# RWKV products stacked in a hybrid encoder layer: b and k in one stationary operand, u and v in one, v centred as it is turned

## The chip, the cores and the metric

The kernel runs on one core of a Trainium2 chip. The metric is the time on the device in microseconds (us) from start to end of one execution of the program; lower is better. The engines are TensorE (PE in the rows, its weight loads PEld), VectorE (DVE), ScalarE (ACT), GpSimd (POOL) and SyncE (SP).

## The reference

One layer of an encoder over 512 tokens of width 2048: a projection feeds three mixers (banded attention, an RWKV-7 time mixing over 16 heads of 64 features, sliding attention with sinks), whose outputs are joined by a projection; then cross attention into 256 tokens and an MLP of width 8192. The change touches the time mixing alone:

```python
def step(state, inp):
    r_t, w_t, k_t, v_t, a_t, b_t = inp
    sa = jnp.einsum('bhij,bhj->bhi', state, a_t)
    state = state * w_t[:, :, None, :] + sa[..., None] * b_t[:, :, None, :] + v_t[..., None] * k_t[:, :, None, :]
    return state, jnp.einsum('bhij,bhj->bhi', state, r_t)
...
y = wkv7_scan(rh, split_heads(decay, B_HEADS), kh, vh, -kk, kk * ah.astype(jnp.float32))
mean = jnp.mean(y, axis=-1, keepdims=True)
var = jnp.mean(jnp.square(y - mean), axis=-1, keepdims=True)
y = ((y - mean) * lax.rsqrt(var + B_GN_EPS)).reshape(b, s, c).astype(pr.dtype) * ln_w + ln_b
bonus = jnp.sum(rh * kh * r_k, axis=-1, keepdims=True) * vh
return (y + bonus.reshape(b, s, c)) * g, v
```

## The kernel before

The large projections are done as three fp32r products (high and low parts) of 128x128 weights with 512 tokens, L1141 to L1143. The input projection runs in 15 groups of 8 units; a unit is 256 rows of the weights. For each unit ScalarE makes the high part (`w_hi`), VectorE the low part (`w_lo`, L713), two units ahead of TensorE. Each group gives three tiles of 128 features in banks 0 to 2 of PSUM. Groups 3 to 10 give r, k and v of a pair of heads (8 pairs, two heads of 64 in the two halves of the partitions).

The RWKV work of the pairs is laid by hand between these products, in the same instruction streams. A unit has three thirds, so a group has 24 positions p. In group g three stages run: `elem` for the pair q = g - 4, `chain` for the pair before it (c), `fin` for the one before that (f). `position(p, g)` issues what belongs to p on each engine, and the engines follow their own streams in order. Ahead of the position's work TensorE issues the chain's step of that third, and behind it six dense matmuls (two tiles, three products each).

`elem` works on chunks of 64 tokens (NC = 8) in fp32. All its small products go through `both` (L1157): the same 64x64 block for the two heads, on the two diagonal quarters of the array; `grams` and `to_tokens` repeat it for 8 chunks. Positions on TensorE: 0 decay and gate projections with 64 rows each (L1189, L1190), 3 turning of v, 8 the bonus sum (L1220), 9 turning of k, 10 gram of k and a, 11 gram of k and r, 12 two grams of a and b, 13 turning of b, 14 gram of b and r and the first product of a blocked inverse, whose levels fill positions 14 to 23 (t, x, xT). VectorE's positions: 6 k decayed (L843) and r decayed, 7 and 8 two reciprocals, `a_dec` (L855), 9 and 10 b (L858, L861), 10 the bonus times v (L866, it frees bank 5 by `bon_ev`), 11 and 12 four masks (L783), 13 start of the inverse, and for `fin` a reciprocal (L887).

`chain` has three steps in a unit: z (L1262, first third, up to two `both`), u (second third, one), then state and y (L1279, last third: two for the new state, then y from u, from v and from the old state). Between them ScalarE copies z and u (L576, L580) and VectorE updates the state (L959, L962). y gathers in bank 7 over the 8 units.

`fin` copies y (L558), takes the mean over a head by a product with a constant (L1194, position 1), subtracts it on VectorE (L819, position 2), squares, takes the variance (L1211) and a gate (L1213, L1214, position 5); GpSimd scales and stores the tile.

After the groups come the attentions, the output projections and the MLP, which the change leaves as they are.

## Time and profile before

| | |
|---|---|
| median of 3 runs | 2764.14 us (2763.07 to 2765.19) |
| profiled execution | 2762.59 us |
| its span, first to last instruction | 2760.9 us |
| mean granted TensorE clock | 0.996 |
| TensorE busy | 2712.9 us, 98% |
| VectorE busy | 1236.4 us, 45% |
| ScalarE busy | 809.3 us, 29% |

The groups with RWKV work take 75.8 us each, from about 143 us to about 820 us. Starts of instructions are in us from the span's start. A matmul's recorded time overlaps with those of its neighbours, so starts are compared. An fp32 matmul shows as two instructions (two passes), each with its own weight load; four small ones in a row ("x4") are the two passes for both heads of one chunk.

### The profile page before, as it was taken

The numbers are of one execution on the slowest core, as the hardware profiler recorded it, in microseconds if no ns is written. First come the engines' busy times: TensorE is split into PE (matmuls) and PEld (weight loads), VectorE is DVE, ScalarE is ACT, GpSimd is POOL, SyncE is SP. The second block draws the span as 40 slices with busy tenths as digits, with TensorE's granted clock in tenths as the row PEclk, the third lists the DMA queues.
The fourth block names the chain that finished last, engine by engine and source line by source line (L and its number), as shares of the span: only waits on it lengthen the run. The fifth ranks groups of instructions, "written<-read, shape, count | busy, mean of one in ns | idle before, by whom it ended". The sixth has DMA issues, their size and how long they took to land.

```text
span 2760.9 us, 44373 instructions
## 1 busy us (share of the span) xinstructions
PE 2712.9 (98%) x18368; PEld 2158.3 (78%) x18368; DVE 1236.4 (45%) x1895; ACT 809.3 (29%) x1333; POOL 132.9 (5%) x237
## 2 busy tenths in 40 slices
PE   9999999999998999998999999999999999999997
PEld 7877777777777766786888888888888888888885
DVE  6266666666435545344433333333333333333333
ACT  5222222222124444243431221312213222122222
POOL 4000111001121100000000000000000000000000
PEclk9999999999999999999999999999999999999998
DMA  4311111111135422221233223322323323323322
GB/s 162 119 60 49 48 48 52 45 50 50 59 108 197 170 79 62 84 88 51 86 98 99 95 97 99 97 93 99 98 92 99 99 92 98 99 92 98 99 94 112
DMA packets 72396, 249.23 MB, mean 90 GB/s; under 512 B 8960, under 2 KB 9088, under 8 KB 71104
## 3 DMA queue, kind: packets, MB, share of 16 engines
q1 hardware_dynamic: 65232, 222.62, 25.3%
q0 software_dynamic: 7024, 24.56, 2.6%
q8 instruction: 109, 1.79, 0.3%
q14 instruction: 31, 0.25, 0.0%
HBM read 236.93 MB, written 10.22 MB: 90 GB/s over the span
## 4 chain that ended last, share of the span: by engine, by line
PE 94%; DVE 3%; issue 1%; DMA 1%; ACT 1%; DVEq 0%; SPq 0%; POOL 0%; ACTq 0%
PE ps L1141 28%; PE ps L1143 26%; PE ps L1142 26%; PE ps L1159 9%; PE ps L1375 1%; PE ps L1354 1%; PE ps L1363 1%; DMA h<-in_mem_turned 1%; PE ps L1153 1%; DVE w_lo L713 0%; PE ps L1214 0%; PE ps L1205 0%; PE ps L1194 0%; PE ps L1211 0%; PE ps L1220 0%
## 5 line engine op out<-in xcount | busy, mean ns | idle before, releaser
L713 DVE TENSOR_TENSOR w_lo<-w_raw,w_hi 128x1024 fp32r<-128x1024 f32 (+2 forms) x440 | 506.0, 1150 | 1143.4 <-ACT w_hi L432 1143.4
L432 ACT ACTIVATE w_hi<-w_raw 128x1024 fp32r<-128x1024 f32 (+2 forms) x440 | 439.0, 998 | 1539.3 <-PE ps L1143 1531.4
L1141 PE MATMUL ps<-act_hi,w_hi 128*128 128x512 f32 x1792 | 730.1, 407 | 1.1 <-DVE w_lo L713 1.1
L1143 PE MATMUL ps<-act_hi,w_lo 128*128 128x512 f32 x1792 | 700.1, 391 | 0.0
L1142 PE MATMUL ps<-act_lo,w_hi 128*128 128x512 f32 x1792 | 699.2, 390 | 0.0
L1141 PE MATMUL ps<-w_hi,mid_hi 128*128 128x512 f32 x1088 | 424.4, 390 | 1.4 <-DVE mid_lo L1087 1.4
L1143 PE MATMUL ps<-w_hi,mid_lo 128*128 128x512 f32 x1088 | 423.3, 389 | 0.0
L1142 PE MATMUL ps<-w_lo,mid_hi 128*128 128x512 f32 x1088 | 423.3, 389 | 0.0
L1141 PEld LDWEIGHTS ps<-act_hi,w_hi 128*128 128x128 f32 x1792 | 336.2, 188 | 93.7 <-issue 12.0
L1143 PEld LDWEIGHTS ps<-act_hi,w_lo 128*128 128x128 f32 x1792 | 336.5, 188 | 72.1
L1142 PEld LDWEIGHTS ps<-act_lo,w_hi 128*128 128x128 f32 x1792 | 336.8, 188 | 68.9 <-issue 6.0
L1141 PEld LDWEIGHTS ps<-w_hi,mid_hi 128*128 128x128 f32 x1088 | 204.3, 188 | 43.5 <-DVE mid_lo L1087 1.6
L1143 PEld LDWEIGHTS ps<-w_hi,mid_lo 128*128 128x128 f32 x1088 | 204.3, 188 | 42.4
L1142 PEld LDWEIGHTS ps<-w_lo,mid_hi 128*128 128x128 f32 x1088 | 204.3, 188 | 41.9
L1020 DVE SCALAR_TENSOR_TENSOR h<-ps,rq,h 128x512 f32<-128x512 f32 x128 | 87.2, 744 | 104.9 <-PE ps L1143 104.9
L1141 PE MATMUL ps<-w_hi,act_hi 128*128 128x512 f32 x256 | 106.2, 415 | 4.2 <-DVE h L1014 3.6
L1143 PE MATMUL ps<-w_hi,act_lo 128*128 128x512 f32 x256 | 100.3, 392 | 0.0
L1142 PE MATMUL ps<-w_lo,act_hi 128*128 128x512 f32 x256 | 100.1, 391 | 0.0
L426 POOL DMA_DIRECT2D w_raw<-in_norm_final x1 | 0.5, 537 | 1614.5 <-DVE w_lo L713 1614.5
L1141 PEld LDWEIGHTS ps<-w_hi,act_hi 128*128 128x128 f32 x256 | 48.0, 187 | 21.4 <-issue 13.3
L1143 PEld LDWEIGHTS ps<-w_hi,act_lo 128*128 128x128 f32 x256 | 48.1, 188 | 10.8
L1142 PEld LDWEIGHTS ps<-w_lo,act_hi 128*128 128x128 f32 x256 | 48.2, 188 | 8.1
(276 smaller groups left out, 2443.3 us busy)
## 6 DMA issues: line engine op xcount, KB each, us to landing
w_raw<-in_w_rest SPq DMA_DIRECT2D x320, 512.0 KB, 3.5
w_raw<-in_w_pairs SPq DMA_DIRECT2D x112, 384.0 KB, 3.0
x_t<-in_x_turned SPq DMA_DIRECT2D x8, 512.0 KB, 8.0
qk<-scr_qkv POOLq DMA_DIRECT2D x16, 256.0 KB, 3.6
h<-in_x POOLq DMA_DIRECT2D x4, 1024.0 KB, 11.1
out<-h SPq DMA_DIRECT2D x4, 1024.0 KB, 4.3
scr_qkv<-pad POOLq DMA_DIRECT2D x15, 256.0 KB, 3.8
w_raw<-in_w_lora SPq DMA_DIRECT2D x8, 288.0 KB, 7.1
```

The lines of the kernel that those rows point to most:

```text
L426: pool.dma_start(gain_out, norm_final.to_broadcast([P, D])).then_inc(s["gout_in"], 16)
L432: return nc.scalar.activation(dst, src, ACT.Copy, scale=scale)
L713: V.tensor_tensor(dst, w_raw[:, slot, 0:dst.shape[-1]], high.bitcast(F32), ALU.subtract).then_inc(s["w_split"], 1)
L1020: V.scalar_tensor_tensor(dst, bank(4 * par + t), rq[:, 1, t:t + 1], dst, ALU.mult, ALU.add).then_inc(s["bank_evac"], 1)
L1141: mm(dst, a_hi, b_hi, start=start, stop=False)
L1142: mm(dst, a_hi, b_lo, start=False, stop=False)
L1143: return mm(dst, a_lo, b_hi, start=False, stop=stop)
L1153: last = nc.tensor.transpose(ps[:, turn_bank(k, kt), t * P:(t + 1) * P], h[:, t, kt * P:(kt + 1) * P], ident[:, :])
L1159: last = mm(dst[hf], lhsT[hf], rhs[hf], start=start, stop=stop)
L1354: mm(ps[:, 4 + n % 2, 0:keys], qk[hf, t % 2, 0, i * P:(i + 1) * P], qk[hf, t % 2, 1, key0:key0 + keys], start=True, stop=True).then_inc(s[ ...
L1363: last = nc.tensor.transpose(ps[:, 6, b * P:(b + 1) * P], att_p[:, n % 4, b * P:(b + 1) * P], ident[:, :])
L1375: last = mm(ps[HALF[half], 7, i * P:(i + 1) * P], vt[:, key0 // P + b, v0:v0 + L], att_pT[:, n % 2, b * P:(b + 1) * P], start=b == 0, stop ...
```

## The change

- The scaled b and k of a chunk lie side by side in `keys_b` (head 0: b, k; head 1: k, b), written by VectorE in two instructions of 64 partitions each. `stacked` takes the 128 columns of a chunk as the stationary operand, with 64 rows for a head, and writes a full bank for each head. So one product with a gives the k-a and the b-a gram, one with r the k-r and b-r gram, and one with the identity turns both.
- The products move: the stacked one with a to position 11 (behind `kt_ready`, `ab_ready`, `bt_ready`, `ss_max` and `bon_ev`), the remaining gram of a and b to 12, turning to 13, the one with r to 14. Positions 9 and 10 of TensorE are empty, and 1 too.
- u and v of a head lie one above the other in `uv` (128 rows). y from both is one product with 128 rows and 64 columns for each head, the new state likewise. v's part of z is issued a unit earlier, at the end of the last third, behind a wait for y's own product (`y_mm`).
- `sy_mm`, behind all of the last third, releases VectorE, which updates the state and copies y of the chunk from PSUM; the next z waits for that copy (`y_ev`).
- v is turned with a matrix that subtracts its mean over the head (`cen2`, one more constant on GpSimd), so y comes out centred; the product for the mean, ScalarE's copy of y and the subtraction are gone.
- ScalarE copies u in two halves, turned v in two halves, and turned b and k in one instruction of 1024 columns.
- Banks: 3 and 4 take the turned tiles and the r grams, 5 and 6 the a grams, 7 the chain.

```diff
-        sg, aa, cs = s2("sig_w", [P, SEQ]), s2("a_gate", [P, SEQ]), s2("cum_sig", [P, SEQ])
+        sg, cs = s2("sig_w", [P, SEQ]), s2("cum_sig", [P, SEQ])
+        keys_b = s2("keys_b", [P, NC, 2, L])
...
+        m_ab = s2("m_ab", [P, SEQ])
+        aa, inv, t_lev = m_ab, cs, sg
...
+        B_TOK, B_W, B_A, B_CHAIN = 3, 5, 6, 7
+
+        def b_part(hd):
+            return keys_b[HALF[hd], :, hd, :]
+
+        def k_part(hd):
+            return keys_b[HALF[hd], :, 1 - hd, :]
+
+        def stack_of(hd):
+            own, other = HALF[hd], HALF[1 - hd]
+            return own, other
...
+            step(nc.gpsimd.tensor_scalar(cen2[:, :], eye2[:, :], 1.0, -1.0 / L, ALU.mult, ALU.add))
...
-                    copy(v_tok[par][:, :], bank(3)).then_inc(s["vtok_ev"], 1)
+                    for hd in range(2):
+                        own, other = stack_of(hd)
+                        last = copy(uv[par][other, hd, :], ps[other, B_TOK, :])
+                    last.then_inc(s["vtok_ev"], 1)
...
-                if p == 9 and elem:
-                    act.wait_ge(s["ktok_mm"], q + 1)
-                    copy(k_tok[par][:, :], bank(3)).then_inc(s["ktok_ev"], 1)
                 if p == 13 and elem:
-                    act.wait_ge(s["btok_mm"], q + 1)
-                    copy(b_tok[par][:, :], bank(3)).then_inc(s["btok_ev"], 1)
+                    act.wait_ge(s["tok_mm"], q + 1)
+                    copy(tok[par][:, :, :].rearrange("p h n -> p (h n)"),
+                         ps[:, B_TOK:B_TOK + 2, :].rearrange("p b n -> p (b n)")).then_inc(s["tok_ev"], 1)
...
-                if fin:
-                    act.wait_ge(s["y_mm"], f + 1)
-                    copy(yb[:, :], bank(7)).then_inc(s["y_ev"], 1)
...
-                        copy(u_s[:, :], ps[:, 6, L:2 * L]).then_inc(s["u_ev"], 1)
+                        for hd, hf in enumerate(HALF):
+                            last = copy(uv[c % 2][hf, hd, part(u)], ps[hf, B_CHAIN, L:2 * L])
+                        last.then_inc(s["u_ev"], 1)
...
+            def masked_pair(dst, b, m):
+                return V.tensor_tensor(dst[:, :, :].rearrange("p h (c t) -> p (h c) t", t=L),
+                                       ps[:, b:b + 2, :].rearrange("p h (c t) -> p (h c) t", t=L),
+                                       over_chunks(m, 2 * NC), ALU.mult)
...
-                if p == 2 and fin:
-                    dve.wait_ge(s["mean_mm"], f + 1)
-                    if f:
-                        dve.wait_ge(s["y_stored"], 16 * f)
-                    V.tensor_tensor(yc[:, :], yb[:, :], bank(3), ALU.subtract).then_inc(s["yc_ready"], 1)
...
-                    V.tensor_tensor(kk_dec[:, :], kp[:, :], g_inv[:, :], ALU.mult).then_inc(s["kt_ready"], 1)
+                    for hd, hf in enumerate(HALF):
+                        last = V.tensor_tensor(k_part(hd), chunks(kp)[hf], chunks(g_inv)[hf], ALU.mult)
+                    last.then_inc(s["kt_ready"], 1)
...
-                    V.tensor_tensor(aa[:, :], aa[:, :], g_inv[:, :], ALU.mult).then_inc(s["bt_ready"], 1)
+                    for hd, hf in enumerate(HALF):
+                        last = V.tensor_tensor(b_part(hd), chunks(aa)[hf], chunks(g_inv)[hf], ALU.mult)
+                    last.then_inc(s["bt_ready"], 1)
...
-                    dve.wait_ge(s["mak_mm"], q + 1)
-                    masked(makT[par], 4, mk_up[:, :]).then_inc(s["mak_ev"], 1)
-                    dve.wait_ge(s["mrk_mm"], q + 1)
-                    masked(mrkT[par], 5, mk_upi[:, :]).then_inc(s["mrk_ev"], 1)
+                    dve.wait_ge(s["gram_a_mm"], q + 1)
+                    masked_pair(m_a[par], B_W, mk_up[:, :]).then_inc(s["gram_a_ev"], 1)
                 if p == 12 and elem:
                     dve.wait_ge(s["mab_mm"], q + 1)
-                    masked(m_ab, 4, mk_lo[:, :]).then_inc(s["mab_ev"], 1)
-                    dve.wait_ge(s["mabT_mm"], q + 1)
-                    masked(m_abT, 5, mk_up[:, :]).then_inc(s["mabT_ev"], 1)
+                    masked(m_ab, B_TOK, mk_lo[:, :]).then_inc(s["mab_ev"], 1)
...
-                    V.tensor_tensor(chunks(invT[par]), chunks(m_abT), over_chunks(mk_1T[:, :]), ALU.mult)
+                    for hd, hf in enumerate(HALF):
+                        V.tensor_tensor(chunks(invT[par])[hf], m_a[par][hf, hd, :].rearrange("p (c t) -> p c t", t=L),
+                                        over_chunks(mk_1T[hf, :]), ALU.mult)
...
-                        dve.wait_ge(s["mrb_mm"], q + 1)
-                        masked(mrbT[par], 3, mk_upi[:, :]).then_inc(s["mrb_ev"], 1)
+                        dve.wait_ge(s["gram_r_mm"], q + 1)
+                        masked_pair(m_r[par], B_TOK, mk_upi[:, :]).then_inc(s["gram_r_ev"], 1)
...
-                        if chain and third == 2 and u < NC - 1:
-                            dve.wait_ge(s["s_mm"], (NC - 1) * c + u + 1)
-                            dst, gl = st_s[:, (u + 1) % 2, :], g_last[:, c % 2, u:u + 1]
-                            if u == 0:
-                                V.tensor_scalar(dst, ps[:, 6, 2 * L:3 * L], gl, None, ALU.mult).then_inc(s["s_ev"], 1)
-                            else:
-                                dve.drain()
-                                V.scalar_tensor_tensor(dst, ps[:, 6, 2 * L:3 * L], gl, st_g[:, :],
-                                                       ALU.mult, ALU.add).then_inc(s["s_ev"], 1)
+                        if chain and third == 2:
+                            dve.wait_ge(s["sy_mm"], NC * c + u + 1)
+                            if u < NC - 1:
+                                dst, gl = st_s[:, (u + 1) % 2, :], g_last[:, c % 2, u:u + 1]
+                                if u == 0:
+                                    V.tensor_scalar(dst, ps[:, B_CHAIN, 2 * L:3 * L], gl, None, ALU.mult)
+                                else:
+                                    dve.drain()
+                                    V.scalar_tensor_tensor(dst, ps[:, B_CHAIN, 2 * L:3 * L], gl, st_g[:, :],
+                                                           ALU.mult, ALU.add)
+                            if u == 0 and c >= 2:
+                                dve.wait_ge(s["y_stored"], 16 * (c - 1))
+                            V.tensor_copy(yy[c % 2][:, part(u)], ps[:, B_CHAIN, 3 * L:4 * L]).then_inc(s["y_ev"], 1)
...
-            def to_tokens(b, src):
+            def stacked(b, rhs):
                 for c in range(NC):
-                    last = both(ps[:, b, part(c)], src[:, part(c)], eye2, True, True)
+                    for hd, hf in enumerate(HALF):
+                        lhsT = keys_b[hf, c, :, :].rearrange("p i t -> p (i t)")
+                        last = mm(ps[:, b + hd, part(c)], lhsT, rhs(hf, c), start=True, stop=True)
+                return last
+
+            def values(b):
+                for c in range(NC):
+                    for hd in range(2):
+                        own, other = stack_of(hd)
+                        last = mm(ps[other, b, part(c)], vv[own, part(c)], cen2[own, :], start=True, stop=True)
                 return last
...
-                if p == 1 and fin:
-                    pe.wait_ge(s["y_ev"], f + 1)
-                    pe.wait_ge(s["xT_ev"], LV * min(q, PAIRS))
-                    mm(bank(3), mean2[:, :], yb[:, :], start=True, stop=True).then_inc(s["mean_mm"], 1)
...
-                if p == 9 and elem:
+                    mm(bank(B_A), ones2[:, :], T1, start=True, stop=True).then_inc(s["bon_mm"], 1)
+                if p == 11 and elem:
                     pe.wait_ge(s["kt_ready"], q + 1)
+                    pe.wait_ge(s["ab_ready"], q + 1)
+                    pe.wait_ge(s["bt_ready"], q + 1)
+                    pe.wait_ge(s["ss_max"], q + 1)
+                    pe.wait_ge(s["bon_ev"], q + 1)
+                    stacked(B_W, lambda hf, c: aT[par][hf, part(c)]).then_inc(s["gram_a_mm"], 1)
...
-                    to_tokens(3, kk_dec).then_inc(s["ktok_mm"], 1)
-                if p == 10 and elem:
-                    pe.wait_ge(s["ab_ready"], q + 1)
-                    pe.wait_ge(s["ss_max"], q + 1)
-                    grams(4, kk_dec, aT[par]).then_inc(s["mak_mm"], 1)
-                if p == 11 and elem:
-                    pe.wait_ge(s["bon_ev"], q + 1)
-                    grams(5, kk_dec, rT[par]).then_inc(s["mrk_mm"], 1)
-                if p == 12 and elem:
-                    pe.wait_ge(s["bt_ready"], q + 1)
-                    pe.wait_ge(s["mak_ev"], q + 1)
-                    grams(4, aT[par], aa).then_inc(s["mab_mm"], 1)
-                    pe.wait_ge(s["mrk_ev"], q + 1)
-                    grams(5, aa, aT[par]).then_inc(s["mabT_mm"], 1)
+                    for c in range(NC):
+                        for hd, hf in enumerate(HALF):
+                            last = mm(ps[hf, B_TOK, part(c)], aT[par][hf, part(c)], b_part(hd)[:, c, :],
+                                      start=True, stop=True)
+                    last.then_inc(s["mab_mm"], 1)
                 if p == 13 and elem:
-                    pe.wait_ge(s["ktok_ev"], q + 1)
-                    to_tokens(3, aa).then_inc(s["btok_mm"], 1)
+                    pe.wait_ge(s["mab_ev"], q + 1)
+                    stacked(B_TOK, lambda hf, c: eye2[hf, :]).then_inc(s["tok_mm"], 1)
...
-                        pe.wait_ge(s["btok_ev"], q + 1)
-                        grams(3, aa, rT[par]).then_inc(s["mrb_mm"], 1)
+                        pe.wait_ge(s["tok_ev"], q + 1)
+                        stacked(B_TOK, lambda hf, c: rT[par][hf, part(c)]).then_inc(s["gram_r_mm"], 1)
+                        pe.wait_ge(s["gram_a_ev"], q + 1)
                         pe.wait_ge(s["inv_init"], q + 1)
                     else:
                         pe.wait_ge(s["x_ev"], (LV - 1) * q + lv)
-                    grams(4, m_abT, inv).then_inc(s["t_mm"], 1)
+                    for c in range(NC):
+                        for hd, hf in enumerate(HALF):
+                            last = mm(ps[hf, B_W, part(c)], m_a[par][hf, hd, part(c)], inv[hf, part(c)],
+                                      start=True, stop=True)
+                    last.then_inc(s["t_mm"], 1)
...
+            def values_into_z(c, u):
+                par = c % 2
+                for hd in range(2):
+                    own, other = stack_of(hd)
+                    last = mm(ps[own, B_CHAIN, 0:L], m_a[par][other, hd, part(u)], uv[par][other, hd, part(u)],
+                              start=True, stop=u == 0)
+                return last
 
             def chain_z(c, u):
                 par = c % 2
-                dst = ps[:, 6, 0:L]
-                if u:
-                    pe.wait_ge(s["s_ev"], (NC - 1) * c + u)
-                last = both(dst, makT[par][:, part(u)], v_tok[par][:, part(u)], True, u == 0)
-                if u:
-                    last = both(dst, aT[par][:, part(u)], st_s[:, u % 2, :], False, True)
-                last.then_inc(s["z_mm"], 1)
+                if NC * c + u:
+                    pe.wait_ge(s["y_ev"], NC * c + u)
+                if u == 0:
+                    values_into_z(c, 0).then_inc(s["z_mm"], 1)
+                else:
+                    both(ps[:, B_CHAIN, 0:L], aT[par][:, part(u)], st_s[:, u % 2, :], False, True).then_inc(s["z_mm"], 1)
...
-                if u < NC - 1:
-                    both(ps[:, 6, 2 * L:3 * L], b_tok[par][:, part(u)], u_s, True, False)
-                    both(ps[:, 6, 2 * L:3 * L], k_tok[par][:, part(u)], v_tok[par][:, part(u)], False, True).then_inc(s["s_mm"], 1)
-                if u == 0 and c:
-                    pe.wait_ge(s["y_ev"], c)
-                dst = ps[:, 7, part(u)]
-                both(dst, u_s, mrbT[par][:, part(u)], True, False)
-                last = both(dst, v_tok[par][:, part(u)], mrkT[par][:, part(u)], False, u == 0)
+                dst = ps[:, B_CHAIN, 3 * L:4 * L]
+                for hd, hf in enumerate(HALF):
+                    last = mm(dst[hf], uv[par][:, hd, part(u)], m_r[par][:, hd, part(u)], start=True, stop=u == 0)
                 if u:
                     last = both(dst, st_s[:, u % 2, :], rT[par][:, part(u)], False, True)
-                if u == NC - 1:
+                if u < NC - 1:
                     last.then_inc(s["y_mm"], 1)
+                    for hd, hf in enumerate(HALF):
+                        mm(ps[hf, B_CHAIN, 2 * L:3 * L], tok[par][:, hd, part(u)], uv[par][:, hd, part(u)],
+                           start=True, stop=True)
+                    pe.wait_ge(s["y_mm"], (NC - 1) * c + u + 1)
+                    last = values_into_z(c, u + 1)
+                last.then_inc(s["sy_mm"], 1)
```

## Rows read from the trace of the kernel before

**Rows 1.** the page, busy time by engine, and the chain that ended last by engine

```profile
PE 2712.9 (98%) x18368; PEld 2158.3 (78%) x18368; DVE 1236.4 (45%) x1895; ACT 809.3 (29%) x1333; POOL 132.9 (5%) x237
...
PE 94%; DVE 3%; issue 1%; DMA 1%; ACT 1%; DVEq 0%; SPq 0%; POOL 0%; ACTq 0%
```

**Rows 2.** who waited for whom on PE: the longest wait of an RWKV product

```profile
PE ps L1159 <- DVE a_dec L855: 1.0, 1, 1.0
```

**Rows 3.** timeline of PE, units 2 and 3: start us, us, engine, line, instruction

```profile
462.50 0.33 PE L1159 MATMUL ps<-u_s,b_tok 64*64 64x64 f32 x4
...
463.13 1.10 PE L1159 MATMUL ps<-r_dec,k_dec 64*64 64x64 f32 x32
464.16 0.51 PE L1141 MATMUL ps<-act_hi,w_hi 128*128 128x512 f32 x1
464.50 0.40 PE L1142 MATMUL ps<-act_lo,w_hi 128*128 128x512 f32 x1
464.73 0.40 PE L1143 MATMUL ps<-act_hi,w_lo 128*128 128x512 f32 x1
```

**Rows 4.** timeline of PE, start of a pair group

```profile
279.61 0.33 PE L1159 MATMUL ps<-v_tok,makT 64*64 64x64 f32 x4
279.87 0.69 PE L1189 MATMUL ps<-lora,prm 64*128 64x512 f32 x1
279.88 0.69 PE L1190 MATMUL ps<-lora,prm 64*128 64x512 f32 x1
```

**Rows 5.** timeline of PEld, the same place

```profile
279.61 0.20 PEld L1159 LDWEIGHTS ps<-v_tok,makT 64*64 64x64 f32 x4 [0.37 <-issue]
279.87 0.18 PEld L1189 LDWEIGHTS ps<-lora,prm 64*128 64x128 f32 x1
...
279.98 0.19 PEld L1189 LDWEIGHTS ps<-lora,prm 64*128 64x128 f32 x1
```

**Rows 6.** timeline of PE, second third of unit 0, with the mean and without

```profile
210.58 0.33 PE L1159 MATMUL ps<-z_s,invT 64*64 64x64 f32 x4
...
212.44 0.33 PE L1159 MATMUL ps<-u_s,b_tok 64*64 64x64 f32 x4
...
434.05 0.33 PE L1159 MATMUL ps<-z_s,invT 64*64 64x64 f32 x4
...
436.74 0.33 PE L1159 MATMUL ps<-u_s,b_tok 64*64 64x64 f32 x4
```

**Rows 7.** groups by line and shape on ACT: one of 64 partitions, one of 128

```profile
L515 ACT ACTIVATE sig_w<-ps,prm 128x512 f32<-128x512 f32 x8 | 5.5, 691 | 8.5 <-DVE prm L805 8.5
...
L572 ACT ACTIVATE lora<-lora 64x512 f32<-64x512 f32 x1 | 0.6, 633 | 3.7 <-DVE lora L944 3.7
```

**Rows 8.** timeline of DVE, units 2 and 3 of the same pair as rows 3

```profile
450.87 0.96 DVE L713 TENSOR_TENSOR w_lo<-w_raw,w_hi 128x768 fp32r<-128x768 f32 x1 [2.95 <-ACT w_hi L432]
...
452.92 0.69 DVE L843 TENSOR_TENSOR k_dec<-k_mod,g_inv 128x512 f32<-128x512 f32 x1
453.52 0.69 DVE L844 TENSOR_TENSOR r_dec<-r_s,g_pad 128x512 f32<-128x512 f32 x1
...
456.02 0.28 DVE L962 SCALAR_TENSOR_TENSOR state<-ps,g_last,state_decayed 128x64 f32<-128x64 f32 x1
456.22 1.75 DVE L850 RECIPROCAL pad<-pad 128x256 f32<-128x256 f32 x1
...
462.07 0.68 DVE L866 TENSOR_TENSOR bonus_v<-ps,v_s 128x512 f32<-128x512 f32 x1
```

**Rows 9.** timeline of DVE and of PE in the first pair

```profile
166.66 0.68 DVE L866 TENSOR_TENSOR bonus_v<-ps,v_s 128x512 f32<-128x512 f32 x1
...
167.40 1.15 PE L1159 MATMUL ps<-r_dec,k_dec 64*64 64x64 f32 x32
```

**Rows 10.** busy time by stretch: PE, PEld, DVE, ACT, POOL, granted clock, DMA

```profile
855.00:863.60 8.60, 5.52 (x26) 4.44 (x27) 6.39 (x8) 2.42 (x3) 4.76 (x9) 1.00 0.76 247
863.60:867.00 3.40, 3.40 (x18) 3.40 (x18) 0.15 (x1) 0.70 (x1) 1.18 (x3) 0.50 0.97 310
```

More of the change, by code:

```diff
@@ L537, in position @@
                     act.wait_ge(s["gate_mm"], f + 1)
-                    copy(gs[:, :], bank(5)).then_inc(s["gate_ev"], 1)
+                    copy(gs[:, :], bank(B_A)).then_inc(s["gate_ev"], 1)
                 if p == 6 and elem:
@@ L575, in _ @@
                         act.wait_ge(s["z_mm"], NC * c + u + 1)
-                        copy(z_s[:, :], ps[:, 6, 0:L]).then_inc(s["z_ev"], 1)
+                        copy(z_s[:, :], ps[:, B_CHAIN, 0:L]).then_inc(s["z_ev"], 1)
                     position(3 * u, g)
@@ L1204, in position @@
                     pe.wait_ge(s["zw_ev"], q + 1)
-                    mm(bank(4), ones2[:, :], T1, start=True, stop=True).then_inc(s["ss_mm"], 1)
+                    mm(bank(B_W), ones2[:, :], T1, start=True, stop=True).then_inc(s["ss_mm"], 1)
                 if p == 5 and fin:
@@ L1219, in position @@
                     pe.wait_ge(s["za_ev"], q + 1)
-                    mm(bank(5), ones2[:, :], T1, start=True, stop=True).then_inc(s["bon_mm"], 1)
-                if p == 9 and elem:
+                    mm(bank(B_A), ones2[:, :], T1, start=True, stop=True).then_inc(s["bon_mm"], 1)
+                if p == 11 and elem:
                     pe.wait_ge(s["kt_ready"], q + 1)
+                    pe.wait_ge(s["ab_ready"], q + 1)
[3 more added lines that the diff above has]
+                    stacked(B_W, lambda hf, c: aT[par][hf, part(c)]).then_inc(s["gram_a_mm"], 1)
+                if p == 12 and elem:
                     pe.wait_ge(s["vtok_ev"], q + 1)
```

74 lines of the change are left out of this document (37 added, 37 removed).

## The prediction

> **What bounds the kernel now.** I read the page's busy shares first, then who waits for whom, then the timelines of TensorE and VectorE over one RWKV pair. TensorE is busy 98% of the span and carries 94% of the chain that ended last [rows 1]. In the RWKV part it waits for VectorE almost never: once 1.0 us, in the first pair [rows 2]. So that part lasts as long as its instruction stream, and an edit is priced in two steps: what it does to the stream, and whether a wait that is now met early becomes late.
>
> The stream is priced from starts of matmuls (their recorded ends overlap). Four instructions are two products 64x64x64 in fp32 (two passes each), one on each diagonal quarter of the array, side by side; I call them a quad. Five quads take 463.13 - 462.50 = 0.63 us, sixteen passes of a gram with the change back to the dense shape 464.16 - 463.13 = 1.03 us [rows 3]; that is 0.117 us for a quad in a run and 0.94 us for the eight quads of a gram. A quad alone between a dense matmul and one of another shape takes 279.87 - 279.61 = 0.26 us [rows 4]: the array runs empty at a change of shape (about 0.09 us) and the first two weight loads are not hidden (0.05 us). Of the 0.26, 0.106 is from the first pass to the second (the four last 0.33 with one pass recorded at 0.22) and 0.148 from there to the next shape; in a run a pass steps on every 0.0585. So **one more change of shape costs 0.14 us**. Weights: the second load of a stationary operand of 128 columns starts 279.98 - 279.87 = 0.11 us after the first; loads of 64 columns, two and two side by side, end 0.20 us after the first starts, those of 128 after 279.98 + 0.19 - 279.87 = 0.30, so 64 columns are worth 0.05 us a load [rows 5]. The load, not the 64 moving columns, sets the step once the stationary operand has 128 columns.
>
> **The change part by part.**
> *Stacked products.* Each has 8 chunks x 2 passes on each half of the rows, the halves side by side as the two projections with 64 rows start together [rows 4]. 16 loads x 0.11 = 1.76 us, and 0.09 for the change of shape: 1.85 us. It replaces two grams, 1.87 us. Gram with a and turning of b and k: -0.03 us each. Gram with r is followed by 64x64 products, so one change of shape more: +0.11. No row shows 128 columns of weights with 64 moving ones in fp32. The price's lower end is 0.06 us a step (loads hidden), 1.07 us a block; a higher one than 0.11 has no row. I take 0.11, because the load row measures this very load. Turning v and the one gram that stays cost what they did.
>
> *Chain.* Per unit z loses a quad (units 1 to 7: -0.117 x 7 = -0.82). The last third had quads in one shape: 5 in units 1 to 6, 0.106 + 8 passes x 0.0585 + 0.148 to the next shape = 0.72 us. It becomes y with 128 rows and 64 columns, state with 64x64, s with 128x64, values into z with 64x64: four quads, each with its own change of shape, 4 x 0.254 = 1.02 us: +0.294 x 6. Unit 0 has three such quads for four in a run: 0.762 - 0.605 = +0.157; unit 7 +0.02. Sum per pair -0.82 + 1.76 + 0.16 + 0.02 = **+1.12 us**, though 15 quads are gone. The unknown is 128 rows x 64 columns: whether its two column halves run side by side as the quarters do. At worst they run in turn, +0.117 on each of 15 such quads, 1.76 us a pair; at best, if neither change of shape costs, -2.8 us a pair. I take side by side and 0.14, the value of each change that the rows show. The wait of TensorE for its own y: the last pass of y starts 0.25 us before the last of s, and a result takes 0.22 to 0.27, so it is met while s runs; its cover is s, and without it it would cost about 0.2 us x 7.
>
> *Mean.* The two fp32 passes over 512 columns go. Third one of unit 0 with them takes 436.74 - 434.05 = 2.69 us, without them 212.44 - 210.58 = 1.86 [rows 6]: **-0.83 us**, eight times.
>
> *VectorE.* k and b are written by two instructions of 64 partitions each. The nearest row (ScalarE, 64x512) takes 0.63 us where one of 128x512 takes 0.69 [rows 7], hardly less for half the partitions; so each added half costs a full step, 0.61 us (453.52 - 452.92 [rows 8]). If it cost half, 0.6 us a pair would come back. The copy of y out of PSUM adds a step of 0.17 (nearest: the state instruction, next start 456.22 - 456.02 = 0.20 [rows 8]). The subtraction of the mean goes, but in unit 0, where VectorE idles later anyway.
>
> **The new wait.** From 450.87, when ScalarE hands over a unit's weights, VectorE works without a pause until the bonus product ends at 462.07 + 0.68 = 462.75 [rows 8]. TensorE's gram in bank 5 starts at 463.13 [rows 3]: a reserve of 0.37 us. After the change this run holds two more halves and a y copy: 0.61 + 0.61 + 0.17 = 1.39 us, so 464.14. TensorE meanwhile arrives earlier, since the first stacked product needs b, k, a and the free bank at once and the two grams that filled thirds 9 and 10 are gone: 463.13 - 0.94 - 0.94 - 2 x 0.117 + 2 x 0.294 + 0.09 = 461.70. The first stacked product starts at 464.2. **Stall 2.5 us a pair.** Behind the wait on TensorE's queue stand the dense matmuls of that third and, through them, everything: nothing else can run. After it I followed the same order with these durations to the end of the pair: mask and turning meet within 0.1 us; the start of the inverse has 3 us, ScalarE's copy of 1024 columns about 1 us, the 3.3 us reciprocal ends 1.5 us before z of unit 5 needs the state. z of unit 3 waits about 0.2 us for y of unit 2, which the same stall contains. The added ScalarE halves (0.2 and 0.6 us) fall before work with more reserve. GpSimd's one more constant is hidden in the first group; SyncE's queue is not passed by anything.
>
> **First pair** (no chain): its gram starts at 167.40; VectorE's bonus product, 166.66 + 0.68 = 167.34 [rows 9], moves by 1.22 to 168.56, so 168.62. Behind it 0.82 (stacked against one gram), -0.94 (one of two masks' grams), +0.77 and +0.95 (turning, r): **+2.8 us**. TensorE is idle here for some 5 us: without the two grams, each with its changes of shape (2 x 1.17), the 1.0 us of [rows 2] and 0.2 of waiting it would come at 163.8.
>
> **Sum.** Pairs 3 to 8: 1.12 - 0.83 + 0.06 + 2.5 = +2.85, six times 17.1. Second pair, without the mean: 3.7. First 2.8. The two groups after, chain and mean once, mean once: +0.29 - 0.83. Together +23.0 us. The profiled execution took 2762.59 us (span 2760.9 and 1.7 around it), 1.5 below the median; the differences were read in it and are added to the median: 2764.1 + 23.0 = **2787 us**.
>
> **The rivals.**
> 1. *Columns in turn* (slower still). The 128x64 products do not overlap: +0.117 x 15 x 8 = 14.0, 2801 us. For: no row has two column halves of one row range together. Against: quarters and row halves do run together [rows 4].
> As a mechanism of this kernel, a load that can't run under a matmul of the same rows would go further: y's four passes would take 4 x 0.11 instead of the 0.165 of two steps with the exposed load, +0.28 x 15 x 8 = 33, 2820 us. Dense matmuls speak against it: all use the same rows and step 0.23 us [rows 3], of which 512 columns at full clock are 0.21, so their load of 0.11 is hidden; it has 0.01 of this rival's chance. The Trainium skill (TensorE: Matmul & The Clock Gate, Part 3) states that rule, that a load overlaps a running matmul only where the row group differs; by it the time would be the 2820, and the trace disagrees.
> 2. *Loads hidden.* A stacked product steps at 0.06: -0.77 x 24 = -18.5, 2768 us, within 0.2%. Against: the 0.11 between loads [rows 5].
> 3. *The wait does not form* (VectorE's run shortens or TensorE is later): without 2.5 x 7 and about 1.2 of the first pair, 2768 us. Against: the two timelines; the reserve is only 0.37 us against 3.2 needed.
> 4. *Only the number of passes counts* (faster). Changes between the small shapes cost nothing and stacked loads are hidden; 15 quads and three grams a pair then really go. The stall stays, since VectorE sets it: +1.07 at the gram, -0.94 for the other gram, -0.117 x 11, -0.83: -2.0 a pair; in all about -16, 2748 us. It decides once a change costs under half of 0.14 and the loads vanish too. Against: every change in the rows costs its 0.09 and the exposed load.
> 5. *Clock.* In the 8.6 us before 863.60 TensorE stood idle for 3.1 us, and then the granted clock was 0.50 for 3.4 us, the level of 1.2 GHz [rows 10], which costs half of 3.4. If each of the eight stalls did so: +13.6, 2801. For: the first pair's 5 us. Against: the others are 2.5 us.
>
> **How the numbers follow.** The forecast has 0.58, rival 1 0.16, 2 0.09, 3 0.05, 4 0.07, 5 0.05. A measurement of this kernel tells 0.2% (5.5 us) from no change. Faster 0.07; within it 0.13 (rivals 2 and 3, at its edge); slower 0.80. The range reaches from rivals 2 and 3 to 1 and 5: 2768 to 2804.
>
> **What would show it.** In the profile after: a wait of TensorE of about 2.5 us for the bonus product's instruction, seven times, and one of 5 us in the first pair; 1.85 us from the first stacked matmul to the next dense one; 1.02 us for the last third of a unit; a unit 0 shorter by 0.8 less 0.2. It is wrong if the stacked block takes near 1.1 us, if y's four instructions take over 0.2 us, or if the bonus product ends before TensorE comes.

## The result and the profile after

The changed kernel takes 2816.07 us (median of 4 runs, 2815.11 to 2817.43), the kernel before beside it 2764.66 us (4 runs, 2763.07 to 2765.67). The ratio is 1.0187, its 95% interval 1.0171 to 1.0203: slower by 51.4 us. The forecast of 2787.0 us had the sign and less than half of the size, and the time lies 12 us above the upper end of its range, 2804. The profiled execution took 2816.0 us (span 2814.3), 53.4 more than the one of before; the medians differ by 51.4, so the traces can be compared as they stand.

Page after: busy time by engine, and the engines' shares of the chain that ended last. They answer to [rows 1].

```profile
PE 2742.7 (97%) x17104; PEld 2173.6 (77%) x17104; DVE 1256.7 (45%) x1959; ACT 828.6 (29%) x1389; POOL 131.0 (5%) x238
...
PE 92%; DVE 5%; ACT 1%; issue 1%; DVEq 1%; DMA 0%; SPq 0%; ACTq 0%
```

TensorE issues 1264 matmuls fewer than before and is busy 30 us longer. Fewer instructions that keep the engine busy longer is the first sign that its clock, or a wider step for each, has to be looked at. VectorE's share of the chain went from 3% to 5%, so there is a wait too. Who waited for whom on TensorE (us in all, times, longest; against [rows 2]):

```profile
PE ps L1193 <- DVE bonus_v L886: 22.5, 8, 5.5
...
PE ps L1181 <- DVE y_cent L985: 2.1, 7, 0.3
```

TensorE's timeline in the fourth pair, from the last quads of unit 2 through the new wait and the three stacked products (start us, us, instruction, and in brackets the idle time ahead of it):

```profile
407.33 0.34 PE L1320 MATMUL ps<-gram_r,uv 128*64 128x64 f32 x4
407.60 0.33 PE L1181 MATMUL ps<-r_dec,state 64*64 64x64 f32 x4
407.86 0.34 PE L1326 MATMUL ps<-uv,tok_bk 128*64 128x64 f32 x4
408.12 0.33 PE L1295 MATMUL ps<-uv,gram_a 64*64 64x64 f32 x4
410.88 3.44 PE L1193 MATMUL ps<-a_dec,keys_b 64*128 64x64 f32 x32 [2.43 <-DVE bonus_v L886]
414.25 0.79 PE L1163 MATMUL ps<-act_hi,w_hi 128*128 128x512 f32 x1
...
420.55 2.00 PE L1193 MATMUL ps<-eye,keys_b 64*128 64x64 f32 x32
422.48 0.50 PE L1163 MATMUL ps<-act_hi,w_hi 128*128 128x512 f32 x1
...
425.12 2.00 PE L1193 MATMUL ps<-r_dec,keys_b 64*128 64x64 f32 x32
427.05 0.45 PE L1278 MATMUL ps<-cum_sig,gram_a 64*64 64x64 f32 x8
```

The same instruction at L1193 takes 3.4 us behind the wait and 1.93 us (422.48 - 420.55, 427.05 - 425.12) ten and fourteen microseconds later. The work is equal; the clock is not. Busy time by stretch around that place (length, PE, PEld, DVE, ACT, POOL, granted clock, DMA):

```profile
404.36:407.77 3.41, 3.41 (x24) 2.23 (x22) 3.16 (x5) 0.58 (x3) 0.00 (x0) 1.00 0.01 2
407.77:411.18 3.41, 0.99 (x18) 0.74 (x17) 3.20 (x7) 0.00 (x0) 0.15 (x1) 1.00 0.39 115
411.18:418.01 6.83, 6.83 (x53) 5.67 (x52) 1.28 (x2) 0.74 (x1) 0.42 (x1) 0.50 0.05 13
418.01:424.00 5.99, 5.99 (x73) 4.77 (x70) 5.58 (x9) 1.79 (x5) 0.00 (x0) 1.00 0.22 66
```

TensorE waits 2.43 us, and just after it resumes the granted clock is 0.50, the level of 1.2 GHz, for 6.83 us. [Rows 10] had such a fall for 3.4 us behind 3.1 us of idle time. Here it is twice as long behind a shorter wait, and it stands in every one of the eight pairs: seven times 6.83 us and once 10.24 us in the first, 58.0 us in all. In the first pair and in the last three the fall begins while TensorE still waits, so TensorE works for 54.3 of the 58.0 us. Half of that, **27 us, is lost**. Another 3.4 us of half clock stand near the start of the program, behind the wait that ends at 35.7 us before and at 35.8 us now; the first RWKV wait (for the shifted v) then ends at 151.0 us for 149.2, 1.8 us late. Of the 53.4 us there remain 53.4 - 27.1 - 1.8 = **24.5 us, where the forecast had 23.0**.

VectorE's timeline in the same pair, which makes the wait (it answers to [rows 8]):

```profile
397.09 0.96 DVE L729 TENSOR_TENSOR w_lo<-w_raw,w_hi 128x768 fp32r<-128x768 f32 x1 [2.96 <-ACT w_hi L448]
...
399.14 1.38 DVE L860 TENSOR_TENSOR keys_b<-k_mod,g_inv 64x512 f32<-64x512 f32 x2
...
403.26 0.21 DVE L985 COPY y_cent<-ps 128x64 f32<-128x64 f32 x1
...
408.63 1.39 DVE L880 TENSOR_TENSOR keys_b<-m_ab,g_inv 64x512 f32<-64x512 f32 x2
410.04 0.69 DVE L886 TENSOR_TENSOR bonus_v<-ps,v_s 128x512 f32<-128x512 f32 x1
```

From 397.09 to 410.73 VectorE does not pause. The run that the prediction followed is there with the two added halves (k at 399.14, b at 408.63) and the copy of y, and it ends 0.15 us before TensorE starts at 410.88.

### The profile page after: what moved, and what is told of

Read it like the earlier page. It is cut to its first block, busy times and chain, and to the rows that moved or that the text cites. A ratio compares the mean times of both kernels' runs of the same rounds, so it can differ in the third digit from the quotient of the medians.

```text
span 2814.3 us, 41967 instructions
## 1 busy us (share of the span) xinstructions
PE 2742.7 (97%) x17104; PEld 2173.6 (77%) x17104; DVE 1256.7 (45%) x1959; ACT 828.6 (29%) x1389; POOL 131.0 (5%) x238
## 4 chain that ended last, share of the span: by engine, by line
PE 92%; DVE 5%; ACT 1%; issue 1%; DVEq 1%; DMA 0%; SPq 0%; ACTq 0%
PE ps L1163 27%; PE ps L1165 25%; PE ps L1164 25%; PE ps L1181 4%; PE ps L1193 2%; PE ps L1278 1%; PE ps L1412 1%; PE ps L1391 1%; PE ps L1400 1%; DVE w_lo L729 1%; PE ps L1175 0%; PE ps L1320 0%; DVE pad L866 0%; DVE pad L868 0%; PE ps L1295 0%
## 5 line engine op out<-in xcount | busy, mean ns | idle before, releaser
L448 ACT ACTIVATE uv<-ps 64x64 f32<-64x64 f32 (+1 forms) x144 | 37.2, 258 | 88.2 <-PE ps L1181 86.8
```

What stands on the lines that cost most here:

```text
L448: return nc.scalar.activation(dst, src, ACT.Copy, scale=scale)
```

## The experiments

Three questions were open. Is it the wait that brings the clock down, or do the new shapes do it, since they fill less of the array? What sets the 1.93 us of a stacked product? And what is the centred v worth alone, so that the rest is the price of stacking?

### 1. The wait alone, from both sides

**e1** runs VectorE's block of position 6 (the product for the bonus, the halves of k) one position earlier, so that it is done before ScalarE hands over the weights of unit 3.

```
-                if p == 6 and elem:
+                if p == 5 and elem:
```

The same replacement stands at both blocks of that position.

> The changed kernel with VectorE's work of position 6 (bonus input, the k halves, decayed r, the last decays) issued at position 5, where it stood idle for about 3 us; nothing else differs. Theory A, clock after stall: the changed kernel lies 51 us over the one before because TensorE's wait for the bonus product (22.5 us in 8 waits) is each time followed by a stretch at half clock (58 us in all at granted 0.5, worth 29 us). This edit shortens VectorE's run before that wait by 2.6 us, so waits and half clock go together: 2816 - 22.5 - 29 = about 2765, granted clock full throughout the RWKV groups. Rival B, the shapes: the stacked and small products keep the array so little busy that the clock falls without a wait as well: the waits go, the eight stretches at 0.5 stay, about 2794.

Measured: 2789.82 us (4 runs, 2789.38 to 2790.07) against 2763.7, ratio 1.0096 (1.0079 to 1.0113). Of the changed kernel's time 26.3 us are gone, about half of what theory A expected, since the edit took away only about half of the waits; the time alone would lie near its rival's 2794, and the trace tells them apart. The waits, one stretch of half clock, and the stretch of the RWKV pairs (second fence: kernel before, changed kernel, e1, in this order):

```profile
PE ps L1193 <- DVE bonus_v L886: 10.5, 8, 4.0
...
479.78:483.19 3.41, 3.41 (x20) 2.38 (x22) 1.19 (x1) 0.62 (x1) 0.00 (x0) 0.50 0.01 1
```

```profile
220.00:840.00 620.00, 620.00 (x8237) 467.23 (x8236) 370.91 (x558) 154.22 (x308) 67.45 (x76) 1.00 0.20 62
220.00:840.00 620.00, 600.87 (x6923) 442.73 (x6922) 378.18 (x614) 165.56 (x359) 51.48 (x58) 0.96 0.16 48
220.00:840.00 620.00, 613.44 (x7017) 451.33 (x7017) 387.87 (x621) 171.94 (x365) 53.34 (x62) 0.98 0.17 52
```

The granted clock of the same stretch is 1.00, 0.96, 0.98. The wait did not vanish: 0.74 us is left in pairs 3 to 8, 2.1 in the second and 4.0 in the first. Half clock sums to 27.3 us: two stretches of 6.8 and four of 3.4, these behind the waits of 0.74 us in pairs 5 to 8; pairs 3 and 4, with the same wait, have none. TensorE works through all but 0.1 us of them. Waits shorter by 12.0 us and half of 54.3 - 27.2 are 25.6 us, against 26.3 measured. For each us of waiting taken away, more than one us of lost clock went with it (12.0 and 13.6).

**e7** leaves VectorE alone and gives TensorE cover: the dense matmuls of the third ahead of the stacked product.

```
+                        late = 3 * u + third == 11
+                        if not late:
+                            position(3 * u + third, g)
...
+                        if late:
+                            position(3 * u + third, g)
```

> The changed kernel with the six dense matmuls of third 11 ahead of that position's stacked product instead of behind it; VectorE unchanged. The first stacked product starts when it did, but 1.6 us of dense work fills the wait, so about 1.1 us of it is left. Theory A: no stretch at half clock in the pairs (except perhaps the first, where some 4 us of wait remain), 2816 - 8 x 1.6 - 24 = about 2779. Rival B: the clock still falls, about 2803.

Measured: 2786.82 us, one run, for the 2779 of theory A and the 2803 of its rival. 0.85 us of wait are left in seven pairs and 4.1 in the first, 10.1 in all; half clock 10.2 us in the first and 3.4 in two of the seven others, 16.1 of them with TensorE at work. Waits shorter by 12.4 and clock by 19.1 are 31.5 us, against 29.3 measured.

**e8** makes both edits, and is the one that leaves the stacked shapes in place without the wait.

> The changed kernel with both edits: VectorE's work of position 6 at position 5, and the dense matmuls of third 11 ahead of its stacked product. All shapes and counts of the change stay, and no wait is left at position 11 but some 2.4 us in the first pair (VectorE's run is 0.7 us short of TensorE in the kernel of e1, and 1.6 us of dense work now lies over it). Theory A (the clock falls where a wait comes on top of the thin stretch, not by the shapes alone): no stretch at 0.5 in pairs 2 to 8; from e1's 2789.8, waits -8, half clock 27.3 us down to some 8, worth -9.5: about 2772. Rival B (the shapes alone bring it down in some pairs): several stretches of 3.4 us stay, 2779 to 2785.

Measured: 2773.06 us (6 runs, 2770.71 to 2774.91) against 2764.32, ratio 1.0033 (1.0021 to 1.0045). The wait is met but in the first pair (2.6 us) and the second (0.5), and from the second pair on there is no half clock; the first still has 6.8 us of it (two stretches, the clock third from the end):

```profile
PE ps L1193 <- DVE bonus_v L886: 3.1, 2, 2.6
...
160.00:220.00 60.00, 57.40 (x752) 45.56 (x751) 35.19 (x52) 10.42 (x18) 0.55 (x1) 0.94 0.16 48
220.00:840.00 620.00, 618.89 (x7053) 457.18 (x7052) 390.33 (x623) 172.84 (x365) 65.01 (x72) 1.00 0.19 57
```

So the shapes alone don't bring the clock down: in none of the seven pairs of this trace. The traced execution is the fastest of the six; whether the slower ones (2774.91 at a mean clock of 0.993, for 0.995) had a fall there is not known.

**e2** adds a wait to e1: VectorE repeats one 128x512 product twice ahead of the bonus product.

```
+                    for _ in range(2):
+                        dve.drain()
+                        V.tensor_tensor(chunks(rT[par]), chunks(rr), g_pad[:, :, 1:1 + L], ALU.mult)
```

> The kernel of e1 with VectorE writing decayed r twice more (same values) before the bonus product, about 1.5 us more in each pair. It asks for the size of wait that brings the clock down. Theory A with a wait of 1.5 us too short to do it: 2765 + 8 x 1.5 = about 2777, clock full. If 1.5 us does it as 2.4 us did: about 2801, seven stretches of 6.8 us at 0.5.

Measured: 2809.99 us, one run. The wait is 2.2 us in five pairs, 2.5 in one, 3.5 in the second and 5.4 in the first (22.3 in all; more than meant, since e1 had 0.74 left), so neither expected time applies. Half clock is back to 6.8 us in seven pairs and 3.4 in the last, 51.2 in all, 50.0 with TensorE at work. Waits 11.8 and clock 11.4 would be 23.2 us over e1; 20.2 were measured, so the rows account for it to 3.0 us.

**e3** puts the same loop, four times, into the kernel before, whose products are all 64x64.

> The kernel before, all its products 64x64, with VectorE writing decayed r four times more (same values) before the bonus product: TensorE should then wait about 2.6 us for it at position 11 in each pair. Theory A (the wait alone brings the clock down, whatever the shapes around it): 2764 + 8 x 2.6 + 7 x 3.4 = about 2810. Rival B (it takes the stacked products as well): 2764 + 21 = about 2785 with the clock full in the pairs.

**e12** does so twice, for a shorter wait.

> The kernel before with VectorE writing decayed r twice more ahead of the bonus product, so that TensorE waits about 1.1 us in each pair, all shapes 64x64. In the changed kernel's shapes a wait of 0.74 us (e1) brought half clock in four of seven pairs and one of 0.85 us (e7) in two of seven. If the stacked shapes make the stretch thinner and so a short wait enough (rival B in part): no fall in the pairs here, 2764 + 8 x 1.1 = about 2773. If the wait alone matters: falls of 3.4 us in several pairs, 2778 or more.

Measured: e3 2804.65 us, one run beside 2763.7. Its waits, the one of the fifth pair, and the fall around it:

```profile
PE ps L1163 <- DVE bonus_v L870: 21.6, 8, 3.2
...
482.87 1.97 PE L1163 MATMUL ps<-r_dec,k_dec 64*64 64x64 f32 x32 [2.60 <-DVE bonus_v L870]
...
482.23:489.05 6.82, 6.18 (x64) 5.02 (x66) 2.26 (x5) 0.95 (x2) 0.56 (x1) 0.50 0.04 13
```

The waits are 3.2 us in the first pair, 2.8 in the fourth and 2.6 in the others. Half clock is 37.5 us: 3.4 in three of the first four pairs, none in the third, 6.8 in the last four; TensorE works for 35.0 of them. 21.6 + 17.5 = 39.1, and 41.0 were measured. **The old shapes lose the clock too when they wait as long**, and a fall of 6.8 us is not a mark of the new ones. e12 took 2774.88 us, one run beside 2764.85: 10.0 more, for 9.5 us of waits. Its waits, one of them in the timeline, and the stretch of the pairs:

```profile
PE ps L1163 <- DVE bonus_v L870: 9.5, 8, 1.7
...
470.21 1.15 PE L1163 MATMUL ps<-r_dec,k_dec 64*64 64x64 f32 x32 [1.06 <-DVE bonus_v L870]
...
220.00:840.00 620.00, 612.18 (x8195) 459.71 (x8194) 379.88 (x573) 154.54 (x309) 64.43 (x70) 1.00 0.18 56
```

No pair shows half clock, behind waits of 1.07 us in six pairs, 1.4 in one and 1.7 in another. With stacked products 0.74 us was followed by it in four pairs of six, and 0.85 in two of seven. That points to the stacked products making a shorter wait enough, but it is not shown, since the length of a wait alone doesn't decide. e1 and e5 (below) issue the same instructions up to the RWKV part, and of the same wait near the start one is followed by half clock and the other is not (e1 above, e5 below):

```profile
36.05 2.04 PE L1170 MATMUL ps<-x_sum,ones 128*128 128x512 f32 x2 [3.32 <-DVE x_sum L760]
...
36.10:39.40 3.30, 3.30 (x6) 1.98 (x7) 1.41 (x2) 0.54 (x1) 2.66 (x12) 0.50 0.64 213
```

```profile
36.35 1.10 PE L1170 MATMUL ps<-x_sum,ones 128*128 128x512 f32 x2 [3.34 <-DVE x_sum L760]
...
36.30:39.70 3.40, 3.35 (x13) 2.46 (x14) 2.33 (x3) 0.63 (x1) 2.05 (x13) 1.00 0.60 223
```

What else decides, and which property of the stacked products would do it (their longer steps, or the changes of shape around them), is not separated by these runs; e7 and e12 are one trace each.

### 2. What sets a stacked product's 1.93 us

**e5** is e1 with half of the moving columns in the product with r. It leaves out the second 32 tokens of each chunk on the side of r in the grams; nothing else is changed.

```
-                        last = mm(ps[:, b + hd, part(c)], lhsT, rhs(hf, c), start=True, stop=True)
+                        last = mm(ps[:, b + hd, c * L:c * L + n], lhsT, rhs(hf, c)[:, 0:n], start=True, stop=True)
```

> The kernel of e1 with only the first 32 of the 64 moving columns in the stacked products with r: the k-r and b-r grams lack half their tokens, so the output isn't the reference's. It asks what sets the 1.93 us of such a product. If the weight load of 128 columns sets the step: the 32 passes still take about 1.9 us. If the moving columns did: about half, 1.0 us.

```profile
410.31 1.98 PE L1193 MATMUL ps<-r_dec,keys_b 64*128 64x32 f32 x32
412.22 0.97 PE L1278 MATMUL ps<-cum_sig,gram_a 64*64 64x64 f32 x26
```

Measured: 1.91 us from the product to the next with 32 moving columns, 1.93 with 64; 2787.16 us in all, one run. Half of the moving data is worth 0.02 us. With 64 columns of weights and the same 64 moving ones the 32 instructions of a gram take 1.03 us [rows 3]. So the steps go by the load of 128 columns. The Trainium skill (TensorE: Matmul & The Clock Gate, LDWEIGHTS) says that a load takes as long as its columns, whatever the rows; the trace agrees for the columns, 16 loads on each half in 1.9 us less the change of shape.

### 3. The centred v alone

**e6** is the kernel before with the centring of v only: v is turned with a centring matrix, the mean's product and subtraction go, and ScalarE copies y straight to where it is stored from.

```
-                if p == 1 and fin:
-                    pe.wait_ge(s["y_ev"], f + 1)
-                    pe.wait_ge(s["xT_ev"], LV * min(q, PAIRS))
-                    mm(bank(3), mean2[:, :], yb[:, :], start=True, stop=True).then_inc(s["mean_mm"], 1)
...
-                    to_tokens(3, vv).then_inc(s["vtok_mm"], 1)
+                    to_tokens(3, vv, cen2).then_inc(s["vtok_mm"], 1)
...
-                    copy(yb[:, :], bank(7)).then_inc(s["y_ev"], 1)
+                    copy(yc[:, :], bank(7)).then_inc(s["y_ev"], 1)
```

> The kernel before with one part of the change alone: v is turned with the centring matrix, the product for the mean, its subtraction on VectorE and its waits are gone, ScalarE copies y straight into the tile that is squared. No product is stacked and nothing else moves. By the prediction's term: -0.83 x 8 = -6.6, no new wait, clock as before: about 2757.5. If the term is false (the third was filled by other work), within 2 us of 2764.

Measured: 2778.01 us (5 runs, 2774.36 to 2780.1) against 2764.32, ratio 1.005 (1.0036 to 1.0064): slower, though work was only taken away. The RWKV part is shorter, by 7.0 us (from the wait for the shifted v, which ends at 149.2 us before and 150.6 in e6, to the first wait behind the part, 855.1 and 849.5). What was lost lies 850 us and more behind that part, in the loop of the MLP, whose work is the same in both: TensorE's waits, one in the timeline, and the stretch of that loop in e6.

```profile
PE ps L1141 <- issue: 12.5, 6, 2.3
...
2048.86 0.50 PE L1141 MATMUL ps<-act_hi,w_lo 128*128 128x512 f32 x1 [2.29 <-issue]
...
1683.00:2620.00 937.00, 924.49 (x4043) 762.92 (x4042) 313.13 (x333) 222.94 (x248) 0.00 (x0) 0.99 0.29 95
```

The same stretch in the kernel before:

```profile
1683.00:2620.00 937.00, 937.00 (x4136) 776.12 (x4135) 321.55 (x343) 231.51 (x260) 0.00 (x0) 1.00 0.30 96
```

Six times, 177 to 178 us apart, TensorE idles 1.8 to 2.3 us with nothing to wait for that the profile names ("issue"), and four of the six are followed by 3.4 us of half clock (the expectation of e10 below says five): 12.5 + 6.8 = 19.3 us, against the 20.5 by which e6 missed its expected 2757.5. The queue that brings instructions (packets, MB, share of 16 engines), e6 and then the kernel before:

```profile
q8 instruction: 163, 2.67, 0.4%
```

```profile
q8 instruction: 109, 1.79, 0.3%
```

The 54 packets more are in this loop, nine in each of six passes, three of them within 10 us around each wait. In the kernel before the last packet starts at 1683 us.

That made a new theory: the edit shortened TensorE's program, the loop's code came to lie elsewhere, and at its new place a piece of it is fetched anew in each pass. **e10** puts 11 products of two passes at the start of TensorE's program, behind the warm-up products, where nobody waits for them; e6 had taken out 8 products of two passes and their waits.

```
+            for i in range(11):
+                mm(ps[:, 7, 0:L], ones[:, :], ones[:, 0:L], start=True, stop=True)
```

> The kernel of e6 (before, with v centred as it is turned and the mean gone) came out 14 us slower than the one before. Its trace shows the mean's time gone from the RWKV groups, and instead six waits of TensorE of 1.8 to 2.3 us in the middle of the MLP loop, once in each pass but the first, put down to nothing but the issue of instructions, with a stretch at half clock behind five of them and instruction DMAs all through the loop, where the kernel before has none from 1683 to 2628 us. Theory C: TensorE's code got shorter by the mean's instructions, and the loop came to lie so that it is loaded anew on every pass. Then 11 small products (44 instructions) added ahead of the first matmul, where TensorE waits anyway, put it back: no waits in the loop, about 2764.3 - 6.6 = 2758. If the place of the code has nothing to do with it: 2778 again.

Measured: **2756.67 us** (7 runs, 2753.8 to 2759.09) against 2764.85, ratio 0.9972 (0.9961 to 0.9983), so 8.2 us faster than the kernel before. No wait named "issue" is left in the loop, the instruction queue is back at 109 packets, and the stretch is whole:

```profile
1683.00:2620.00 937.00, 937.00 (x4135) 775.86 (x4135) 323.55 (x345) 231.87 (x260) 0.00 (x0) 1.00 0.29 96
```

Adding 11 useless products saved 21 us over e6. The two kernels differ in nothing else, and they come out of the RWKV part within 0.3 us of each other (849.5 and 849.8), so it isn't a shift in time: that the place of the code causes the waits is shown. The fetches in each pass are there in the two kernels with the waits (e6, e9) and in neither of those without (e10, e11 below). Where the boundaries lie, and why those fetches come late, is not.

**e9** and **e11** add the edit of e1 to e6 and to e10, to take away the 1.0 us wait of [rows 2].

> The kernel of e6 with VectorE's work of position 6 at position 5 as in e1. In the kernel before TensorE met that work late only in the first pair (1.0 us for a_dec and 0.2 behind it), so about -1.2: 2756.3. If it brings waits elsewhere (VectorE is later for the low part of a unit's weights), no gain or a loss.

> The kernel of e9 (e6 with VectorE's work of position 6 at position 5) with the same 11 small products. Theory C: about 1.2 us under e10, 2757. If the place of the code has nothing to do with it: 2775 as e9.

Measured: e9 2775.33 us (5 runs, 2772.55 to 2775.9), ratio 1.0039 (1.0025 to 1.0053); the wait of the first pair is 0.3 us for 1.0, and the six of the loop are there (13.4 us in all), so it misses its expected 2756.3 as e6 did. e11 2756.9 us (6 runs, 2753.43 to 2758.74), ratio 0.9969 (0.9957 to 0.9981), which can't be told from e10. The fastest kernels run, e10 and e11, are the kernel before with v centred and its loop code in place, without stacking.

## Why the prediction was right or wrong

- **Stacked product, forecast 1.85 us at a step of 0.11.** Right: 1.93. e5 shows the reason given, the load. Rival 2 (loads hidden) is out.
- **Four quads of a last third, 1.02 us.** Right: in the rows above 407.33, 407.60, 407.86 and 408.12 are 0.27 + 0.26 + 0.26, and in the unit before that, from the first of the four to the next shape, it is 400.81 - 399.76 = 1.05 in all. A change of shape costs 0.15 where 0.14 was taken. Rival 1 is out: its column halves in turn would make 0.254 + 0.117 = 0.37 us of a 128x64 quad, and it takes 0.26 to 0.27. The rule of the Trainium skill that stood beside it (TensorE: Matmul & The Clock Gate, Part 3), by which a load overlaps a running matmul only where the row group differs, would make 0.254 + 0.28 = 0.53 us of it, and the trace disagrees: both column halves have the same rows. Rival 4 is out by the same rows.
- **Mean, -0.83 us a pair.** Right: a full group takes 74.88 us in e10 for 75.74 before, 0.86 less. In the medians e10 gains 8.2 us, where 6.6 were forecast.
- **VectorE.** Right: each half of 64 partitions costs a full step, the copy of y 0.2.
- **The new wait, 2.5 us in seven pairs and some 5 in the first.** Right, in place, cause and size: 2.43 and 5.5 us. That z of the next unit waits for y showed as 0.3 us, seven times. Rival 3 is out.
- **The clock (rival 5), chance 0.05 and 13.6 us.** This is the step that failed, twice: the sum had nothing for it, and the rival that had it was priced too low. The chance rested on "the others are 2.5 us", read against one fall behind 3.1 us in [rows 10]; e2 and e3 show that 2.2 and 2.6 us are enough in nearly every pair, e1 and e7 that 0.74 and 0.85 can be. And the price took one row's 3.4 us for the length of every fall; it was 6.8 in seven pairs and 10.2 in the first. By these lengths it is 27 us (29 if TensorE had worked through all of them) instead of 13.6, and the forecast with it 2814 to 2816.
- **What the prediction could have seen.** The 3.1 us of [rows 10] are the end of one wait and the whole of another: 3.37 us up to 855.12, then 4.8 us of dense work at full clock, then 2.96 us up to 862.88, and the fall behind that. A third idle time of that size, 2.67 us up to 35.7, has no fall either:

```profile
851.75:855.12 3.37, 0.00 (x1) 0.04 (x1) 3.37 (x10) 1.88 (x6) 0.00 (x0) 1.00 0.00 0
855.12:859.92 4.80, 4.79 (x20) 3.65 (x20) 2.59 (x5) 0.42 (x1) 4.26 (x9) 1.00 0.59 155
```

One case for and two against make a chance of about one in three, not 1 in 20. Since the stall was forecast to recur eight times at the same place of the same loop, the eight falls also were nearer to one event than to eight: the range had to reach to the sum with all of them.
- **Small sums.** The chances of rivals 2 and 3 add up to 0.14, those of a slower kernel to 0.79; the prediction has 0.13 and 0.80. It changes nothing.

The parts can be read from the full groups, those that start with pairs 4 to 7, from the first decay product of one to that of the next. The kernel before takes 75.74 us, e10 74.88 (506.44 to 581.32), e8 76.43 (438.08 to 514.51) and the changed kernel 82.0 to 82.4. So stacking with its wait met costs 1.55 us a group, where the sum had 1.12 + 0.06; three stacked products longer by 0.08 and six last thirds longer by 0.03 explain the 0.37 over it (0.42). The wait adds 2.43 and the clock what is left, 3.1 to 3.6 us, about half of 6.83. Over the whole kernel e8 and e10 leave 2773.06 - 2756.67 = 16.4 us between them, of which 3.1 are the waits left and 3.4 the clock in the first pair; some 10 us are the work itself (8 by the two traces), where the sum's terms make 9.4. The waits of 22.5 us and the clock of 27 come on top. Without the last of either, e8 would take 2773.06 - 3.1 - 3.4 = 2766.6 by this estimate, still not under the 2764.3 of the kernel before.

## What to carry to other kernels

Price a stall of TensorE twice: once for its length, and once for the clock behind it, which here cost more than the stall (27 us against 22.5); and where the stall recurs in a loop, let the range hold the case that all of them do it. Stacking operands to 128 columns saves instructions but not time where the load of the columns, and not the moving side, sets the step (here with 64 moving columns in fp32), and each product of its own shape costs 0.15 us here. When an edit that only removes work makes a kernel slower, look for waits named "issue", in loops far from the edit too, and at the packets of the instruction queue, before the edit itself is blamed.

## What the runs showed of the hardware that was not expected

- The granted clock fell to 0.50 for 6.8 us around waits of 2.2 to 2.6 us in most pairs of the changed kernel, e2 and e3 (3.4 us in some, and none in the third pair of e3). Around stacked products it fell for 3.4 us behind 0.74 us in four pairs of six (e1) and behind 0.85 us in two of seven (e7); waits of 1.07 to 1.7 us between 64x64 products were not followed by a fall in any of eight pairs (e12). The Trainium skill (TensorE: Matmul & The Clock Gate, Why this matters for your kernels) advises against idle gaps of over about 3 us between bursts; these runs disagree with that as a safe bound.
- The same wait can go either way: 3.32 us in e1 with 3.4 us of half clock behind it, 3.34 us in e5, at the same place of the same code, with none.
- Code that is the same ran 12.5 us of waits and 6.8 us of lost clock slower for its place in TensorE's program (e6), with 163 instruction packets instead of 109, and 11 products of padding took that back (e10).
- 32 matmuls with half of the moving columns (32 for 64) took 1.91 us for 1.93 with loads of 128 columns (e5).
